# Turning fourteen modulation vectors on VectorE and ScalarE instead of TensorE in a two-block transformer kernel

## The reference

```python
c_act = jax.nn.silu(c)
for i in range(DEPTH_2):
    mod = c_act @ w_ada[i] + b_ada[i]
    sh1, sc1, g1, sh2, sc2, g2 = jnp.split(mod, 6, axis=-1)
    h = modulate(rmsnorm(x, norm_mix_g[i]), sh1, sc1)
    m = fourier_mixer(h, ...) if i == 0 else retention_mixer(h, ...)
    x = x + g1[:, None, :] * m
    h = modulate(rmsnorm(x, norm_ffn_g[i]), sh2, sc2)
    x = x + g2[:, None, :] * swiglu(h, w_ffn_in[i], w_ffn_out[i])
shf, scf = jnp.split(c_act @ w_ada_final + b_ada_final, 2, axis=-1)
return modulate(rmsnorm(x, final_norm_g), shf, scf)
```

## Time and profile before

| | |
|---|---|
| median of 3 runs | 1541.06 us (1540.83 to 1541.74) |
| the profiled execution | 1540.15 us, of which the span is 1538.2 us |
| mean clock granted to TensorE | 0.999 of full |
| PE / PEld busy | 99% / 83% |
| DVE / ACT / POOL busy | 51% / 41% / 57% |
| weights and steps read | 259 chunks and 112 steps of 512 KB, 131 GB/s over the span |
| the costliest groups, busy | POOL L423 868.9 us; PE L1785, L1788, L1789 (a tiles) 479.2, 476.6, 476.7 us; ACT L455 269.9 us; DVE L995 149.1 us |

### The profile page before, as it was taken

How to read it: one execution, slowest core, us unless ns; L and a number is a source line. 1 busy time by engine, 2 the same in 40 slices (tenths; PEclk the granted TensorE clock), 3 DMA queues, 4 the chain that set the end, 5 groups by cost and what they waited for, 6 DMA issues and landing times.

```text
span 1538.2 us, 21352 instructions
## 1 busy us (share of the span) xinstructions
PE 1526.9 (99%) x7242; PEld 1276.9 (83%) x7242; DVE 786.8 (51%) x1176; ACT 632.4 (41%) x1038; POOL 876.3 (57%) x1040
## 2 busy tenths in 40 slices
PE   9999999999999999999999999999999999999997
PEld 7888888898888888888888888888889888888886
DVE  7887787876654544541554435356257454011113
ACT  7444444674533333323444334253345333122223
POOL 6555557556577766775454535526435766555551
PEclk9999999999999999999999999999999999999999
DMA  7544455335355555542232322213312553222321
GB/s 247 178 145 165 167 192 191 110 110 178 122 180 205 196 190 181 199 150 96 101 103 69 108 69 94 95 52 96 95 55 83 205 205 123 96 96 95 95 82 55
DMA packets 58267, 202.99 MB, mean 132 GB/s; under 512 B 6496, under 2 KB 8544, under 8 KB 58208
## 3 DMA queue, kind: packets, MB, share of 16 engines
q1 hardware_dynamic: 56912, 198.87, 37.8%
q10 hardware_dynamic: 1296, 3.30, 0.6%
HBM read 200.05 MB, written 2.10 MB: 131 GB/s over the span
## 4 chain that ended last, share of the span: by engine, by line
PE 78%; POOL 11%; issue 9%; ACT 0%; DMA 0%; DVE 0%; SPq 0%; POOLq 0%; DVEq 0%; ACTq 0%
PE banks L1785 21%; PE banks L1789 21%; PE banks L1788 21%; POOL w_lo L423 11%; PE banks L2270 2%; PE banks L2269 2%; PE banks L2266 2%; PE banks L1801 2%; PE banks L1804 2%; PE banks L1805 2%; PE banks L2306 1%; PE banks L2304 1%; PE banks L2305 1%; PE banks L2293 0%; PE banks L2292 0%
## 5 line engine op out<-in xcount | busy, mean ns | idle before, releaser
L423 POOL TENSOR_TENSOR w_lo<-w_raw,w_hi 128x256 fp32r<-128x256 f32 x1028 | 868.9, 877 | 627.8 <-ACT w_hi L455 627.7
L455 ACT ACTIVATE w_hi<-w_raw 128x1024 fp32r<-128x1024 f32 x257 | 269.9, 1057 | 582.6 <-PE banks L1785 518.8
L1785 PE MATMUL banks<-a_hi,w_lo 128*128 128x512 f32 x1224 | 479.2, 391 | 0.1
L1789 PE MATMUL banks<-a_hi,w_hi 128*128 128x512 f32 x1224 | 476.7, 389 | 0.0
L1788 PE MATMUL banks<-a_lo,w_hi 128*128 128x512 f32 x1224 | 476.6, 389 | 0.0
L1785 PEld LDWEIGHTS banks<-a_hi,w_lo 128*128 128x128 f32 x1224 | 230.1, 188 | 47.6 <-issue 0.8
L1789 PEld LDWEIGHTS banks<-a_hi,w_hi 128*128 128x128 f32 x1224 | 229.8, 188 | 47.8
L1788 PEld LDWEIGHTS banks<-a_lo,w_hi 128*128 128x128 f32 x1224 | 229.9, 188 | 47.3 <-issue 0.2
L1785 PE MATMUL banks<-b_hi,w_lo 128*128 128x512 f32 x562 | 219.6, 391 | 0.0
L1789 PE MATMUL banks<-b_hi,w_hi 128*128 128x512 f32 x562 | 218.8, 389 | 0.0
L1788 PE MATMUL banks<-b_lo,w_hi 128*128 128x512 f32 x562 | 218.8, 389 | 0.0
(11 more groups left out here) (300 smaller groups left out, 1708.4 us busy)
## 6 DMA issues: line engine op xcount, KB each, us to landing
w_raw<-in_W SPq DMA_DIRECT2D x258, 512.0 KB, 3.5
ada_raw<-in_ADA SPq DMA_DIRECT2D x112, 512.0 KB, 4.2
X<-in_XT SPq DMA_DIRECT2D x8, 256.0 KB, 6.3
scr<-in_DECAY ACTq DMA_DIRECT2D x4, 448.0 KB, 3.9
out<-X SPq DMA_DIRECT2D x7, 256.0 KB, 2.2
w_raw<-in_W SPq DMA_DIRECT2D x2, 256.0 KB, 3.9
scr<-in_PT ACTq DMA_DIRECT2D x1, 512.0 KB, 4.8
scr<-in_ROPE ACTq DMA_DIRECT2D x1, 512.0 KB, 4.5
```

Of the source, the lines that this page charges most:

```text
L423: pool.tensor_tensor(w_lo[:, c % RING, part], w_raw[:, c % RING, part], w_hi[:, c % RING, part].bitcast(fp32), ALU.subtract).then_inc(wlo, 1)
L455: act.activation(w_hi[:, c % RING, :], w_raw[:, c % RING, :], ACT.Copy).then_inc(whi, 1)
L1785: mm = pe.matmul(out, lo, x_hi, start=first, stop=False)
L1789: mm = pe.matmul(out, hi, x_hi, start=False, stop=last)
```

## The change

All 14 vectors are finished by fold, move and collect; PE's 32 transposes and 8 column products (16 in the trace) go, and with them one `aux` turn per head. The area in which a vector is turned depends on the vector (`turned_home`). In the heads, the fold stands at the head's end on DVE, and the moves and the collect of that vector stand in the next head: on ACT between the cast of chunk c0+10 and `weights_hi(2)`, on DVE behind `weights_lo(3)`. The first head moves and collects an area of zeros into an extra row ahead of `mod`; vector 3 is moved and collected in the output product at n == 1, vector 4 in `fout`. The steps of vector 5 leave the Fourier mixer: from there on each vector is made 8 steps later. Layer 0's first `up` becomes straight code on ACT and DVE, and vector 11's steps, which were in `up0b`, stand in `down0b`, two behind each of the first four residuals. SP loads the steps accordingly: none beside chunks 44 to 72, then one behind each of chunks 73 to 128 (before: 73 to 120).

```diff
@@ SP
-            straight(*[0] * 8, 1, 1, 0, 0, 0, 1, 1, 1, 1, 1, 1)
-            assert pos[1] == 6 * KD
             until(CH["up0a"] + 10)
-            turns(6 * KD // 4, 4, 1)
+            turns(7 * KD // 4, 4, 1)
@@ ACT
+            def ada_move(g, at=flat):
+
+                _, part, quads = turned_home(g)
+                quads = quads.rearrange("p (f b) -> p f b", b=4)
+                act.wait_ge(ada_folded, at("vector", g + 2))
+                for b in range(4):
+                    for q in range(4):
+                        ins = act.activation(quads[32 * q:32 * q + 32, :, b], part[32 * b:32 * b + 32, q:32:4], ACT.Copy)
+                ins.then_inc(ada_moved, 1)
...
                 exps(at, 3)
                 split_w(at, c0 + 10)
+                ada_move(-1, at)
                 weights_hi(at, 2)
                 weights_hi(at, 3)
...
             for n in range(8):
+                if n == 1:
+                    ada_move(NH - 1)
                 if n != 3:
                     split_w(flat, c0 + n + 4)
@@ DVE, a head
                 weights_lo(at, 3)
+                ada_collect(-1, at)
                 ada(at, 1)
                 scale_gate(at, 7)
...
-                ada_out(A0 + 6, 0, at, 4)
+                ada_fold(0, at)
@@ DVE, ple and the Fourier mixer
-                if m == 2:
-                    ada_out(AUX["ada4"], 4)
...
-            ada(k=3)
+            ada_fold(4)
             for n in range(8):
                 if n >= 3:
                     if n == 3:
-                        dve.wait_ge(aux_free, AUX["ada4"] + 1)
+                        ada_collect(4)
+                        dve.wait_ge(ada_made, 6)
@@ DVE, down0b
                     elif layer == 0:
-                        dve.wait_ge(ada_made, 7)
+                        dve.wait_ge(ada_made, 9)
                         scale_columns(3, col("mix", KD, KD), 7)
-                        residuals(t, range(KD - 1), g0 + 5, v)
+                        for m in range(KD - 1):
+                            residuals(t, (m,), g0 + 5, v)
+                            if m < 4:
+                                ada(k=2)
@@ PE
-                if n == 17:
-                    ada_turn(at, A0 + 6, 0, 4)
...
-                    if m == 3:
-                        ada_columns(flat, AUX["ada4"], 4)
```

More of the change, by code:

```diff
@@ L105 @@
 _c = 0
-for _name, _n in (("pre", 1), ("body", 7 * NH), ("post", 1), ("ada4", 1), ("ple", 1), ("four", 1), ("fshift", 1), ("edge", 1),
+for _name, _n in (("pre", 1), ("body", 6 * NH), ("post", 1), ("ple", 1), ("four", 1), ("fshift", 1), ("edge", 1),
                   ("ffn0", 1), ("rnorm", 1),
@@ L595, in _ @@
             with act.Fori(0, NH) as i:
-                at = At(i, chunk=8, slot=32, tile=8, bank=2, aux=7, unit=4, one=1, two=2, eight=8)
+                at = At(i, chunk=8, slot=32, tile=8, bank=2, aux=6, unit=4, one=1, two=2, eight=8, vector=1)
                 split_w(at, c0 + 4)
@@ L824, in swiglu @@
                         up_body(flat, c, t, j)
-                    if layer == 0:
-                        n_pairs, g = (n_hid // 2 - first) // 2, 5 if first else 9
+                    if layer == 0 and first:
+                        for k in range(1, n_hid // 2):
+                            up_body(flat, c + 4 * k, t + 4 * k, j + 2 * k, 5 if k == 3 else None)
+                        ada_move(6)
+                    elif layer == 0:
+                        n_pairs, g = (n_hid // 2 - first) // 2, 8
                         with act.Fori(0, n_pairs) as i:
@@ L1275, in _ @@
             base = linked[0]
-            per_link = 1 + 4 * 3 + 4 + 1 + 1
+            dve.memset(turned_home(0)[1], 0.0).then_inc(ada_folded, 1)
+            per_link = 1 + 4 * 3 + 4 + 1 + 2
             with dve.Fori(0, NH) as i:
-                at = At(i, chunk=8, tile=8, bank=2, aux=7, unit=4, one=1, two=2, eight=8, link=per_link,
-                        ada=8, adaslot=64)
+                at = At(i, chunk=8, tile=8, bank=2, aux=6, unit=4, one=1, two=2, eight=8, link=per_link,
+                        ada=8, adaslot=64, vector=1)
                 for n in range(2):
@@ L1957, in split_stats @@
                 pe.matmul(aux, ones_r[:, :], b_hi[:, slot, :], start=False, stop=True).then_inc(aux_ready, 1)
-            def ada_columns(at, u, g):
-                pe.wait_ge(ada_sum, at("ada", KD * (g + 1)))
-                pe.wait_ge(aux_free, at("aux", u))
-                for f in range(KD):
-                    mm = pe.matmul(aux[:, f:f + 1], ada_acc[:, f * P:(f + 1) * P], ones[:, 0:1], start=True, stop=True)
-                mm.then_inc(aux_ready, 1)
-            def ada_turn(at, u, g, bank):
-                pe.wait_ge(ada_sum, at("ada", KD * (g + 1)))
-                pe.wait_ge(aux_free, at("aux", u))
-                for f in range(KD):
-                    out = banks[:, bank if f < KD // 2 else 7, f % 4 * P:(f % 4 + 1) * P]
-                    mm = pe.transpose(out, ada_acc[:, f * P:(f + 1) * P], ident)
-                mm.then_inc(aux_ready, 1)
             pe.wait_ge(const, 1)
@@ L2046, in body_tail @@
                     split_stats(at, A0 + 5, 8)
-                if n == 17:
-                    ada_turn(at, A0 + 6, 0, 4)
-            per = dict(chunk=8, tile=8, bank=2, aux=7, unit=4, one=1, two=2, eight=8, ada=8)
+            per = dict(chunk=8, tile=8, bank=2, aux=6, unit=4, one=1, two=2, eight=8, ada=8)
             def first_hook(n):
```

105 lines of the change are left out of this document (45 added, 60 removed).

## The result

The changed kernel takes 1555.98 us in the median of 5 runs (1555.39 to 1557.68), beside 1540.86 of the kernel before (1540.72 to 1541.74): a ratio of 1.0099, 95% interval 1.0086 to 1.0113. It is 15 us slower, where the prediction had 11. On the scale of the medians shown before this is 1541.06 x 1.0099 = 1556.3, just above the range's upper end of 1556.0.

What follows compares the result with a forecast made beforehand. PE, busy 99% of the span, was taken to bound the kernel. Heads +2.7, ple -0.1, down0b's queue +6.8 and the clock +1.8 sum to +11.2 on 1540.15, 1551.3, put at 1552.2 us for the median; range 1545.5 to 1556.0.

Steps and rivals of the forecast that it cites:

- +2.7: Four heads, net: PE gains 3.5 us from the transposes but waits 6.2 us for ACT's 16 copies.
- the 0.09: Heads, ACT: taken off the copies' 3.60 us because copies start without waiting for a PSUM read.
- The covers behind it: Heads, DVE: `o_sum_lo` slack falls from 1.0 to 0.2, the fold hides behind PE; costed at nothing, at most 0.5 each.
- 718.8 + 3.6 + 1.06 + 3.7: down0b: chunk 124's issue, landing, ACT's cast and POOL's pieces give 727.2; PE stands 6.8 us.
- The clock: Behind down0b's stall: TensorE restarts at 1.2 GHz, costing between 0 and 2.1 us, taken as 1.8.
- -0.1: ple: 1.79 us fewer on PE become wait; only one DVE addition of 0.1 is left.
- zero, with chunk 37's cast as the closest: Mixer, folds and moves elsewhere: cost nothing beside PE's products; chunk 37's cast in the output product comes 3.6 later.
- That chain doesn't move: ple: DVE's X update waits for ACT's `rinv`, so the squares, casts and chunk 46 stay put and PE's gain becomes wait.
- the clock did not stay up: Rival, behind down0b's stall: the clock does not fall, saving 1.8 us, 1550.4; chance 0.15.
- the waits did not fail to come: Rivals: no wait in the heads, 1546.0, chance 0.06; SP's queue in down0b doesn't bind, 1543.6, chance 0.07.
- the transposes did not cost their whole length: Rival, heads: transposes don't overlap, so removing them gains 8.3 us instead of 3.5, 1547.4; chance 0.02.
- More waits than I count: Rival: `o_sum_lo` and chunk 37 are passed and POOL's pieces stretch to 4.4, about 1555; chance 0.05.

Runs made afterwards that it cites:

- experiment 2: Changed kernel, but in each head the 16 copies stand ahead of the cast of chunk c0+10 on ACT: 1550.92 us.
- 10: Changed kernel, but in each head 4 of the 16 copies stand ahead of the cast of chunk c0+10 and 12 behind it: 1553.36 us.
- Experiment 3: Changed kernel, with 30 products of 128 columns into an unused area on PE ahead of its wait for chunk 124: 1554.76 us.
- experiment 4: Changed kernel, but vector 3's 16 copies and the collect stand one cast later in the output product, at n == 2: 1554.58 us.
- 1: Changed kernel, but the first two steps of vector 11 stand ahead of down0b's first residual on VectorE: 1545.81 us.
- 5: Changed kernel, but in down0b SP loads step 90 behind chunk 124 and each later step one chunk later: 1549.78 us.
- 9: Changed kernel, but once step 88 is done SP issues chunk 124's load first and those of steps 90 and 91 behind it: 1555.13 us.
- 6: Changed kernel with steps ahead of down0b's first residual, heads' copies ahead of the cast, output product's copies and collect one cast later: 1537.99 us, 0.9982 of the kernel before.

## Why the prediction was wrong

The direction was right, and so were the place and the releaser of the two large waits; the sum was 3.9 too small, and the range ended 0.3 too low. Of the 3.9, 1.1 is chunk 124's landing, 1.0 the clock, 1.3 the wait in the gate and the output product, and 0.2 the heads; the rest is within the spread of the runs.

**Heads, right.** +2.7 predicted, +2.9 by the steps (6.1 - 3.2). Experiments 2 and 10 show the mechanism: copies' time less slack. Two terms of the prediction were a little off: the transposes gave 0.80 a head, not 0.88, and the 0.09 that it took off the copies isn't there, since `weights_hi(2)` starts 3.62 behind the first copy. The covers behind it held: `o_sum_lo` is ready at 119.96 and PE reads it at 120.44.

**down0b, right in mechanism, mis-sized.** "718.8 + 3.6 + 1.06 + 3.7" was the sum. The issue came out right (724.48, less the 5.6 by which all had shifted by then, is 718.9), but by luck: step 88 took 0.74, not 1.2, and the 0.6 that step 90's load takes on SP ahead of the chunk was not in the sum. Cast and POOL were right. Landing was the term that failed: 4.5 in place of 3.6, because step 90's load goes out 0.6 ahead of the chunk. The median of part 6 is over all 258 loads, and most of them have no step's load right ahead; the 26 of the kernel before that do have 4.6 in the median, and that was the price to take. The 4.72 of the earlier trace rows, kept as the upper end, is no landing at all: it is how long ACT was idle. That chunk was issued at 361.28 and its cast began at 365.27, 4.0 later. With 4.5 the wait is 7.9, and with the 5.7 of experiment 2 it is 9.1.

**The clock, right in mechanism, mis-sized.** 1.8 was taken and 2.8 measured (1.5 to 3.0 in other profiles). Thirteen pitches stand behind the wait before the pace of 0.23 is back, 5.7 us in all, where I had bounded it with the 4.23 of the program's start. That start is no bound for a restart. What the clock costs varies, and not with the length of the wait: 2.8 behind 7.9, 1.5 behind 9.1. What sets it, no run here shows. Experiment 3 shows that the 2.8 are the clock's. The Trainium skill, "TensorE: Matmul & The Clock Gate", section "HAM oscillation", had the mechanism: a wait on a DMA, and the next burst begins cold. The trace agrees: the wait goes back to chunk 124's load, and the granted clock is 0.50 when PE starts again.

**The output product and ple, wrong by 1.3.** "-0.1" for ple and "zero, with chunk 37's cast as the closest" for the output product. I counted what PE would lose if chunk 37 were late, and it was not late. The step that failed is what stands behind it on the other queues: the copies wait for the fold as well (2.27), so SP's loads and DVE's last steps slipped, and POOL's low parts with them. "That chain doesn't move" was wrong: in ple its first work went slower on DVE, 1.31 in place of 0.69, while POOL was working beside it, and 0.69 again in experiment 4, where POOL was done. That makes 0.6 to 0.7 of the 1.3; the 0.5 in the output product showed in two profiles of eight. The gate's chain was read rightly as the one that takes back ple's 1.7, but only its end at chunk 46 was looked at; PE first waits 1.6 for the squares.

**Not foreseen at all: a clock that falls in some executions.** The two waits in the gate, with five matmuls between, were enough for it in five of the nine profiles that have them without products put in. In those five (experiments 1, 2, 3, 5, 9) the jump at the squares was 2.1 to 2.2; in the four where the clock stayed (the changed kernel, 4, 6, 10) 1.2 to 1.9. It costs 0.9 to 2.9. That is also where the kernel's larger spread may come from, 2.3 between its runs in place of 1.0. The runs of experiments 1 and 10 bear it out, since the slower ones have the lower mean clock. For the changed kernel it is not shown: its slowest run (1557.68) has 0.994, but so has one at 1555.89, and the others have 0.995.

The rivals: the clock did not stay up, the waits did not fail to come, and the transposes did not cost their whole length (0.80 for eight, 0.10 each). "More waits than I count" named the right place, chunk 37, by the wrong mechanism. That its 1555 is nearest to the measured time is luck.

## What to carry to other kernels

On a queue that works in order, a load that waits for a semaphore holds back every load behind it: ask of each moved step not only when it is done but what is queued behind the load that waits for it. Price a load by loads with the same neighbours, not by the median of all. Time saved on the bounding engine counts only if what it waits for next is not tied to another engine; here 1.7 us became wait and, where the clock fell, loss. And the place of a piece of work within an engine's program decides more than its length: two lines exchanged gave 5 us, two steps placed earlier 10, and the change as a whole turned from 15 us slower into 2.9 faster.

## What was unexpected of the hardware

Behind a wait of 7.9 us TensorE ran at 1.2 GHz for 5.7 us of continuous work, at a pitch of 0.43, before it was back at 2.4 GHz; behind one of 9.1 us, in another profile, for 3.1 us only. Dummy products in the wait, ones by ones into an unused area, kept the clock up, and the wait was no longer for it (7.93). Two shorter waits of about 1.6 to 2.0 and 0.6 us, with five matmuls between them, were followed by half clock in five of nine profiles. Chunk 124's load of 512 KB, issued 0.6 us behind another, landed in 4.4 to 5.7 us, and in 3.6 when it went first. VectorE's 128x512 operations took 0.69 us, and up to 1.31 with GpSimd at work beside them; GpSimd's 128x256 pieces took 0.72, and 1.71 to 1.77 where one began during VectorE's work on a step.
